# Two layers of a hybrid decoder: router logits in the cross output projection, expert rows gathered and scattered by index, x and y moved by thirds

## The reference

```
x += W_out[pool | MLA | GLA] of RMSNorm(x)
x += CrossAttn(RMSNorm(x))          # 4 heads of 128 over 256 memory tokens, then w_xo
x += HierMoE(RMSNorm(x))
y  = RMSNorm(x)                      # after the last layer

HierMoE(h):
  g_logit = h @ w_rg + b_rg ; group = argmax over 4
  e_logit = h @ w_re + b_re ; the 8 experts of that group ; top 2
  gate    = softmax(g)[group] * top_p / sum(top_p)
  rows of each expert in blocks of 128
  out     = (silu(xb @ w_eg[e]) * (xb @ w_eu[e])) @ w_ed[e]    # 1024 -> 256 -> 1024
  y       = sum over a token's two slots of gate * out
```

## Time and profile before

| | us |
|---|---|
| median of 3 runs (lowest, highest) | 3118.25 (3117.82, 3120.85) |
| the profiled execution | 3119.8 |
| its span, first to last instruction | 3118.0 |
| PE busy in the span | 2694.3 (86%) |
| DVE, ACT, POOL busy | 1239.8 (40%), 748.5 (24%), 335.0 (11%) |
| expert blocks of a layer, first gate/up to the last down, layer 0 | 1122.0 to 1507.8 |

### The profile page before, as it was taken

One profiled execution on the slowest core, in us unless ns is written; L12 is line 12 of the kernel. 1 busy time (PEld: TensorE's weight loads), 2 busy tenths in 40 slices (PEclk: granted clock), 3 DMA queues, 4 the chain that ended last, 5 costly groups with the idle time before them and its releaser, 6 DMA issues.

```text
span 3118.0 us, 33197 instructions
## 1 busy us (share of the span) xinstructions
PE 2694.3 (86%) x12924; PEld 1624.3 (52%) x12924; DVE 1239.8 (40%) x2242; ACT 748.5 (24%) x1513; POOL 335.0 (11%) x499
## 2 busy tenths in 40 slices
PE   7999977789999669999599998668899984999994
PEld 4645556456567334444365455555666752444443
DVE  3155557341313613333343455663223334333325
ACT  1124445231012111111211344443200211111112
POOL 0003324100000010000200232321000002000002
PEclk9999985799999779999799999758899996999996
DMA  9310000331140279998420100005213105899954
GB/s 368 119 27 19 8 31 1 146 129 68 33 156 14 88 307 354 359 356 345 158 70 11 27 13 5 31 4 215 103 34 122 68 22 200 317 360 356 351 230 167
DMA packets 79382, 451.69 MB, mean 145 GB/s; under 512 B 17246, under 2 KB 17884, under 8 KB 67932
## 3 DMA queue, kind: packets, MB, share of 16 engines
q1 hardware_dynamic: 46524, 311.84, 27.0%
q0 software_dynamic: 20368, 101.72, 8.5%
q10 hardware_dynamic: 12352, 36.25, 2.9%
HBM read 361.77 MB, written 84.66 MB: 143 GB/s over the span
## 4 chain that ended last, share of the span: by engine, by line
PE 67%; DVE 18%; ACT 5%; POOL 4%; issue 3%; DMA 2%; ACTq 0%; DVEq 0%; POOLq 0%; SPq 0%
PE ps L612 18%; PE ps L1187 15%; PE ps L1127 4%; PE ps L649 4%; PE ps L729 4%; DVE arena L2206 4%; DVE arena L2200 3%; PE ps L741 2%; PE ps L906 2%; PE ps L757 2%; PE ps L818 2%; DVE arena L1642 2%; PE ps L707 2%; POOL slots L2345 1%; PE ps L955 1%
## 5 line engine op out<-in xcount | busy, mean ns | idle before, releaser
L612 PE MATMUL ps<-arena,ring 128*128 128x352 f32 x1920 | 574.0, 462 | 2.3 <-ACTq L400 1.0
L612 PEld LDWEIGHTS ps<-arena,ring 128*128 128x128 f32 x1920 | 366.4, 191 | 207.7 <-issue 5.0
L1187 PE MATMUL ps<-arena 128*128 128x512 f32 x1024 | 463.6, 606 | 11.6 <-DVE arena L2200 5.6
L1187 PEld LDWEIGHTS ps<-arena 128*128 128x128 f32 x1024 | 191.9, 192 | 245.8 <-issue 225.1
L1205 PE MATMUL ps<-arena 128*128 128x512 f32 x512 | 232.2, 596 | 3.2 <-ACT arena L1572 3.2
L2205 DVE TENSOR_SCALAR arena<-arena 128x256 f32<-128x256 f32 x64 | 18.8, 294 | 496.9 <-ACT arena L1568 496.9
L729 PE MATMUL ps<-arena 96*128 96x512 f32 (+3 forms) x384 | 149.7, 500 | 0.0
L2016 DVE TENSOR_TENSOR x<-x,ps 128x1056 f32<-128x1056 f32 x32 | 40.1, 1255 | 274.8 <-PE ps L612 199.0
L1205 PEld LDWEIGHTS ps<-arena 128*128 128x128 f32 x512 | 93.0, 191 | 97.6 <-issue 93.9
L1579 ACT ACTIVATE arena<-ps 128x1024 f32<-128x1024 f32 x64 | 65.6, 1024 | 259.9 <-PE ps L1205 259.9
L2358 POOL DMA_INDIRECT arena<-slots,dest x36 | 37.5, 1041 | 814.7 <-ACTq L400 804.3
(11 more groups left out here) (375 smaller groups left out, 3742.8 us busy)
## 6 DMA issues: line engine op xcount, KB each, us to landing
arena<-in_w_e SPq DMA_DIRECT2D x64, 3072.0 KB, 11.1
arena<-slots SPq DMA_DIRECT2D x64, 512.0 KB, 4.4
slots<-arena ACTq DMA_DIRECT2D x64, 512.0 KB, 10.3
ring<-in_ring SPq DMA_DIRECT2D x56, 512.0 KB, 3.7
slots<-arena POOLq DMA_DIRECT2D x1, 24576.0 KB, 81.4
arena<-in_mem_k SPq DMA_DIRECT2D x16, 512.0 KB, 6.5
arena<-in_mem_v SPq DMA_DIRECT2D x16, 512.0 KB, 9.9
x<-in_x SPq DMA_DIRECT2D x1, 4224.0 KB, 15.7
```

The costliest lines, as they stand in the source:

```text
L612: mm = pe.matmul(ps[:, (j % 2) * NCH + c, 0:CH], ring[:, slot, (j % per) * units + k, :], src[:, k, tok], start=k == 0, stop=k == units - 1)
L1187: mm = pe.matmul(ps[:, 2, :], xb_t[:, p, k, :], w_e[j][:, k * 512:(k + 1) * 512], start=k == 0, stop=k == KT - 1)
```

## The change

1. The router's logits are accumulated within the cross output projection. After tile j of x is final, ACT writes its square and, scaled by the gain g_ffn alone, the tile itself to `xn`; after the projection matmuls of tile j+1 PE adds tile j's part to the logits (`logits`). The root of the mean square is found once per token, and the logits are multiplied by it afterwards on DVE, where the bias is added too. Barrier 8 is gone.
2. The rows are transposed unnormalised, and ACT multiplies by the token's factor as it copies them to `xr`. SP writes them in token order to a DRAM tensor `xrow`; nothing waits for the routing there.
3. Nine more matmuls give each token's place with the counts of earlier tiles included. Two comparisons and 18 matmuls then turn token -> slot into a table slot -> token, `idx`: for each block a column of 128 row numbers; a slot that holds nobody gets a number outside the bounds, and that row isn't moved.
4. In the expert blocks POOL gathers the rows of a block from `xrow` by that table (`gather`, in place of `load_x`) and scatters y to `yrow` (`scatter`, in place of ACT's store); `release` tells ACT that a y buffer has been written out. `slots`, its zero fill and the waits for it are gone.
5. In the combine stage the two rows of a token lie at fixed places of `yrow`, so SP loads them with plain DMAs, one per tile.
6. x is loaded and y stored in three parts, one per chunk of tokens, and each chunk's work waits only for its own part (the masks load with the second, rope with the third).

```diff
-        slots = nc.dram_tensor("slots", [NBLK * CAP, D], F32).ap()
+        xrow = nc.dram_tensor("xrow", [TOK, D], F32).ap()
+        yrow = nc.dram_tensor("yrow", [2 * ROWS, D], F32).ap()
...
+            def x_load(c):
+                sp.dma_start(x[:, :, chunks[c][1]], ins["x"][:, :, chunks[c][1]]).then_inc(x_moved[c], 16)
             sp.dma_start(consts[:, :], ins["consts"]).then_inc(setup, 16)
-            sp.dma_start(rope[64:96, :, :], ins["rope"]).then_inc(setup, 16)
-            sp.dma_start(lmask_f, ins["lmask"]).then_inc(setup, 16)
-            sp.dma_start(x[:, :, :], ins["x"]).then_inc(setup, 16)
             sp.dma_start(pages[:, :], ins["pages"]).then_inc(setup, 16)
+            x_load(0)
+            sp.dma_start(lmask_f, ins["lmask"]).then_inc(x_moved[1], 16)
+            x_load(1)
+            x_load(2)
+            sp.dma_start(rope[64:96, :, :], ins["rope"]).then_inc(x_moved[2], 16)
...
-                def load_x(p, n):
-                    sp.dma_start(xb[:, p, :], slots[bass.ds(CAP * n, CAP), :]).then_inc(xb_full[p], 16)
...
+                sp.wait_ge(states_stored, 16 * (DB + 6 + 2 * GH))
+                sp.wait_ge(lin_done, IN_MT + OUT_MT + XK_MT + XQ_MT + 1)
                 load_w(0, 0)
-                sp.wait_ge(ssq_ready, 3 * NCH)
-                load_w(3, 3)
-                sp.wait_ge(rows_ready, 1)
-                load_x(0, 0)
-                load_x(1, 1)
-                sp.wait_ge(xr_done, NT + 1)
-                load_w(1, 1)
-                load_w(2, 2)
-                for n in range(2):
-                    sp.wait_ge(tx_done, n + 1)
-                    load_x(n, n + 2)
+                for t in range(NT + 1):
+                    m = P if t < NT else ND
+                    sp.wait_ge(xr_evac, t + 1)
+                    sp.dma_start(xrow[t * P:t * P + m, :], xr[0:m, t % 4, :]).then_inc(row_moved[t % 4], 16)
+                sp.wait_ge(ssq_ready, 2 * NCH + 1)
+                sp.wait_ge(tabled, 1)
+                for j in range(1, 4):
+                    load_w(j, j)
...
-                        sp.wait_ge(tx_done, n + 3)
-                        sp.sem_inc(turn, 1)
-                        load_x(j % 2, n + 4)
                         sp.wait_ge(dn_done, n + 1)
                         sp.sem_inc(turn, 1)
                         load_w(j, n + 4)
...
+                for t in range(NT + 1):
+                    m = P if t < NT else ND
+                    if t >= 4:
+                        sp.wait_ge(c_ready, t - 3)
+                    sp.dma_start(yg[0:m, t % 4, :, :], yrow.rearrange("(s r) d -> r s d", s=2)[t * P:t * P + m, :, :]).then_inc(row_moved[t % 4], 16)
...
+            for c, tok in chunks:
+                sp.wait_ge(norm_ready, c + 1)
+                sp.dma_start(outs["y"][:, :, tok], xn[:, :, tok]).then_inc(x_moved[c], 16)
+            for c in range(NCH):
+                sp.wait_ge(x_moved[c], loaded[c] + 16)
...
+                def logits(k):
+                    pe.wait_ge(xg_ready, k + 1)
+                    if k == 0:
+                        pe.wait_ge(wr_full, 16)
+                    for c, tok in chunks:
+                        mm = pe.matmul(lg_at[c], w_r[:, k, :], xn[:, k, tok], start=k == 0, stop=k == KT - 1, skip_group_check=True)
+                        if k == KT - 1:
+                            mm.then_inc(lg_done, 1)
                 for j in range(XO_MT):
                     for c in range(NCH):
                         if j == 0 and c == NCH - 1:
                             x_back(NT)
                         x_out(j, c)
-                stage_end(pe, 8)
+                    if j >= 1:
+                        logits(j - 1)
+                logits(KT - 1)
                 pe.wait_ge(sq_added, 2)
...
+                for t in range(NT + 1):
+                    m = P if t < NT else ND
+                    mm = pe.matmul(ps[0:m, 2, t:t + 1], xsum[:, t * P:t * P + m], ones[:, 0:1], start=True, stop=True)
+                mm.then_inc(ssq_ready, 1)
...
+                for t in range(6):
                     rows_of(t)
                 pe.wait_ge(both_ready, 1)
...
+                pe.matmul(ps[:, 4, 0:(NT + 2) * NE], con("below"), both.rearrange("p t e -> p (t e)"), start=True, stop=False,
+                          skip_group_check=True)
+                for t in range(NT + 1):
+                    mm = pe.matmul(ps[:, 4, (t + 1) * NE:(NT + 2) * NE], ones,
+                                   both[:, t, :].unsqueeze(1).broadcast_to([P, NT + 1 - t, NE]), start=False, stop=t == NT,
+                                   skip_group_check=True)
+                mm.then_inc(ranked, 1)
+                for t in range(6, NT + 1):
                     rows_of(t)
+                for s_ in range(2):
+                    pe.wait_ge(hot_ready, s_ + 1)
+                    for t in range(NT + 1):
+                        mm = pe.matmul(ps[:, 5, 0:NBLK], hot_row[:, s_, t, :], hot_blk[:, s_, t, :], start=s_ + t == 0,
+                                       stop=s_ == 1 and t == NT)
+                mm.then_inc(tabled, 1)
...
+                    act.wait_ge(lin_evac, IN_MT + OUT_MT + XK_MT + XQ_MT + k + 1 + 2)
+                    act.activation(xsum if k == 0 else xsq[:, k % 2, :], x[:, k, :], ACT.Square, scale=D ** -0.5).then_inc(sq_ready, 1)
+                    act.activation(xn[:, k, :], x[:, k, :], ACT.Copy, scale=gain("g_ffn", k)).then_inc(xg_ready, 1)
                 for c, tok in chunks:
                     act.wait_ge(lg_done, c + 1)
...
+                    act.activation(lgt[0:NR, tok], lg_at[c], ACT.Copy).then_inc(lg_evac, 1)
+                act.wait_ge(ssq_ready, 2 * NCH + 1)
+                act.activation(rstd_t[:, 0:NT], ps[:, 2, 0:NT], ACT.Sqrt, bias=EPS).then_inc(std_ready, 1)
+                act.activation(rstd_t[0:ND, NT:NT + 1], ps[0:ND, 2, NT:NT + 1], ACT.Sqrt, bias=EPS).then_inc(std_ready, 1)
...
+                for t in range(NT + 1):
                     m = P if t < NT else ND
                     act.wait_ge(xr_done, t + 1)
                     if t >= 4:
...
                     b = 0 if t % 2 == 0 else 6
-                    act.activation(xr[0:m, t % 4, :].rearrange("p (a n) -> p a n", a=2), ps[0:m, b:b + 2, :], ACT.Copy).then_inc(xr_evac, 1)
...
+                    act.activation(xr[0:m, t % 4, :].rearrange("p (a n) -> p a n", a=2), ps[0:m, b:b + 2, :], ACT.Copy,
+                                   scale=rstd_t[0:m, t:t + 1]).then_inc(xr_evac, 1)
...
-                def send_y(n, p, sent):
+                def keep_y(n, p):
                     act.wait_ge(dn_done, n + 1)
-                    act.wait_ge(y_sent[p], sent + 16)
+                    act.wait_ge(y_out, n + 1)
                     act.sem_inc(turn, 1)
                     act.activation(y_sb[:, p, :].rearrange("p (a n) -> p a n", a=2), ps[:, 4:6, :], ACT.Copy).then_inc(dn_evac, 1)
-                    act.wait_ge(dn_evac, n + 1 + 1)
-                    act.sem_inc(turn, 1)
-                    act.dma_start(slots[bass.ds(CAP * n, CAP), :], y_sb[:, p, :]).then_inc(y_sent[p], 16)
...
+                for j in range(KT):
+                    dve.wait_ge(lin_done, IN_MT + OUT_MT + XK_MT + XQ_MT + j + 1)
+                    xs = x[:, j, :].rearrange("p (c n) -> p c n", c=NCH)
+                    dve.tensor_tensor(xs, xs, ps[:, (j % 2) * NCH:(j % 2 + 1) * NCH, 0:CH], ALU.add).then_inc(lin_evac, 1)
+                    if j >= 2:
+                        add_xsq(j - 1)
+                add_xsq(KT - 1)
...
+                for s_ in range(2):
+                    step(dve.tensor_tensor(hot_blk[:, s_], blk_f[:, s_, :].unsqueeze(2).broadcast_to([P, NT + 1, NBLK]),
+                                           iota[:, 0:NBLK].unsqueeze(1).broadcast_to([P, NT + 1, NBLK]), ALU.is_equal))
+                    step.mark(dve.tensor_tensor(hot_blk[:, s_], hot_blk[:, s_], row_id[:, s_, :].unsqueeze(2).broadcast_to([P, NT + 1, NBLK]),
+                                                ALU.mult))
+                    step.sync()
+                    dve.tensor_tensor(hot_row[:, s_], row_f[:, s_, :].unsqueeze(2).broadcast_to([P, NT + 1, P]),
+                                      iota.unsqueeze(1).broadcast_to([P, NT + 1, P]), ALU.is_equal).then_inc(hot_ready, 1)
+                dve.wait_ge(tabled, 1)
...
+                dve.tensor_copy(idx, table).then_inc(idx_ready, 1)
...
-            pool.dma_start(slots.rearrange("(p n) (f c) -> p (n f) c", p=P, c=512),
-                           zeros.unsqueeze(1).broadcast_to([P, NBLK * CAP // P * 2, 512])).then_inc(slots_clear, 16)
...
+                def gather(n):
+                    pool.indirect_dma_start(xb[:, n % 2, :], None, xrow, bass.IndirectOffsetOnAxis(ap=idx[:, 0, n:n + 1], axis=0),
+                                            bounds_check=TOK - 1, oob_is_err=False).then_inc(xb_full[n % 2], 16)
+                def scatter(n):
+                    pool.wait_ge(dn_evac, n + 1 + 1)
```

(58 more changed lines are left out.)

177 lines of the change are left out of this document (64 added, 113 removed).

## The result

| | us |
|---|---|
| before, median of 4 runs beside it (lowest, highest) | 3118.03 (3116.57, 3120.85) |
| changed, median of 4 runs (lowest, highest) | 3544.95 (3539.55, 3548.68) |
| ratio, 95% interval | 1.136 (1.134 to 1.138) |
| changed, the profiled execution and its span | 3547.88, 3546.0 |

The change is slower by 427 us. 3383 had been forecast, within 3265 to 3550.

A forecast was written before the change was run, and what follows sets the result against it. PE, busy 86% of the span, was taken as the bound, its own in the expert blocks. Sum: 3119.8 + 307 (expert blocks) - 30 (logits, table, first gather) - 6 (start) - 6 (end) - 2 (combine) = 3383 us, range 3265 to 3550.

The forecast's parts named there:

- the clock's case: Expert blocks: rival that PE's clock falls after each stall, each costing 2.6 us more, 151 in all, 3534; chance 0.13.
- The rule of the queue: Expert blocks: gather(n+1), behind scatter(n-2) on POOL, cannot issue before block n-2's down matmuls end; 5.3 us a block, 58 times.
- T: Start of a block's gate/up matmuls; the forecast counts times within a block from it, the old period being 11.77 us.
- The expert blocks: Both layers: late gathers lengthen the period from 11.77 to 17.05 us, 58 x 5.3 = +307; this forecast had chance 0.47.
- the middle of two rows: Expert blocks: gather landing taken as T+12.15, between the y store's T+11.55 and the x load's T+12.8.
- the crowded engines: Expert blocks: rival that filled rows crowd on some DMA engines, gather landing at T+12.8, 58 x 5.9 = 342, 3418; chance 0.17.
- Logits in the projection, table, first gather: Last residual add to first gate/up: logits within the projection, row scatters gone; -15 us a layer, -30 in all (-10 to -50).
- Combine: Combine stage: one SP load a tile replaces two POOL issues, last scatter takes POOL's path; -2 us in all (-6 to +4).
- Start: Kernel start: with x in thirds, two squares and sums are done before the last third's; -6 us (-3 to -9).
- end: Kernel end: only a third of the 11.8 us from the y store's issue is left; -6 us (-4 to -8).
- Zero fill: nothing: First projection: removing the zero fill gains nothing, as its 352 matmuls take 104.40 us with or without it.

The follow-up runs named there:

- The later scatter: Changed kernel with POOL's queue in the order gather(n+2), scatter(n-2), the scatter two blocks later: 3088.04 us, 0.991 of the kernel before.
- the run with spread rows: Changed kernel with slot r of a block in partition 2r, then the odd ones, instead of partition r: 3466.72 us, ratio 1.110.
- the filled wait: Changed kernel with six more 128x512 matmuls a block between gate/up and the transposes of x, output unchanged: 3421.51 us (one run).
- The run with the first weights held back: Scatter two blocks later, plus SP loading weights of blocks 1 to 3 only after gathers 0 and 1 land: 3057.03 us, ratio 0.982.

## Why the prediction was right, and where it was not

**The direction and the mechanism held, the size did not.** 3545 us lies only 5 us inside the range, whose upper end was there for the clock's case alone, with a chance of 0.13; the forecast itself was 162 us too low. The rule of the queue (a gather behind a scatter that waits for y cannot leave before T) and its times were right to 0.2 us: gather from T+3.2 to T+4.3, forecast T+3.1 to T+4.1; 58 stalls. The later scatter took it all away.

**The expert blocks were mis-sized: +447, not +307.** Two things, and both were listed as rivals. I took the landing from the middle of two rows, T+12.15; it came at the upper end, T+12.7, and the transposes began at T+12.95, 0.7 later than by my sum. I had charged the crowded engines as a case of their own, and the run with spread rows shows that they take part. The larger error was the clock. The argument against it, that a gap of 2.63 us had left the clock at 1.00, was an argument from a short gap to one twice as long; the filled wait shows 2.1 us of the 7.7 per block to be the clock alone. The rival's price of 2.6 a stall was near the 2.4 measured, but it is the transposes and down that pay it; gate/up, 7.03 us, runs at 1.00. The rivals were priced as if only one could be true; crowded engines and clock together, 342 + 151, would have been +493, and the truth lies between. From the rows: 326 us of stalls and 139 for the slower matmuls behind them are 465. Against these 18 too many stand 7 us less of idle time ahead of gate/up (11.6 before, 4.6 now) and 7 less of gate/up itself (busy 463.6 before, 456.3 now); the last few are not accounted for.

**Logits in the projection, table, first gather: -15 a layer was -12.3 in layer 0.** The parts were off both ways. The changed kernel's timeline:

```profile
1034.74 1.25 DVE L2154 TENSOR_TENSOR x<-x,ps 128x1056 f32<-128x1056 f32 x1 [6.18 <-PE ps L1138]
...
1045.56 0.50 DVE L2165 TENSOR_TENSOR arena<-arena 128x324 f32<-128x324 f32 x1
...
1079.20 1.10 POOL L2391 DMA_INDIRECT arena<-xrow,arena  x1 [162.98 <-DVE arena L2237]
...
1101.06 1.97 PE L1212 MATMUL ps<-consts,arena 128*128 128x128 f32 x8 [23.71 <-POOLq L409]
```

With the start's 5.2 us added back, the last residual add comes at 1039.9: the projection grew by 7, not 13 (six logit matmuls take 1.37 us there, not 6 x 0.307). Logits are ready at 1051.3, forecast 1056. The indices took 32 us from there (33), so gather 0 left POOL at 1079.2, where 1091 less the start's 5 had been forecast. From the last add to the first gate/up the timelines have 19.3 us less, where 28 had been named. The 7 us at the gather and 3 more were lost again behind it: the first gathers were forecast to land in at most 10.4 us and took up to 20.3, beside three weight loads at once, and gate/up began at 1104.5. The run with the first weights held back won some 30 us of that for the two layers.

In layer 1 the gain after the last add is nearly the same (-17.9, against -19.3 in layer 0), but 5 us are lost in the middle of the layer, where no code was changed: the granted clock is 0.88 in the changed kernel between 2306 and 2506 us and 0.91 in the matching 200 us before. The run with the later scatter, with the same code there, is 3 us shorter from the end of the first combine to the last add of layer 1. The cause was not followed up.

**Combine: -2 was +9.** I had priced the loads and not what comes before them (layer 1):

```profile
3466.23 1.02 ACT L1610 ACTIVATE arena<-ps 128x1024 f32<-128x1024 f32 x1 [3.90 <-PE ps L1238]
3468.03 0.97 POOL L2397 DMA_INDIRECT yrow<-arena  x1 [4.18 <-ACT arena L1610]
3477.58 2.12 SPq L586 DMA_DIRECT2D arena<-yrow  x4
```

From the start of ACT's last copy of y to the first load are 11.35 us; in the kernel before 5.3 to the first gather (5.4 in layer 0). By the first transposes of the combine 4.7 and 4.5 us of the difference are left (layers 0 and 1), which are the 9.

**Start -5.2 and end -5.7 were right in size (-6, -6).** "Zero fill: nothing" was right for the kernel before, where everything waited for all of x anyway and the 352 matmuls take 104.40 us with and without it. But the start's gain exists only because the fill is gone. The two terms are one.

## What to carry to other kernels

When a queue issues two kinds of work, ask of each entry what the entry ahead of it waits for: a store that waits for the end of a block must not stand ahead of the load that the next block needs, and moving it back costs nothing where the buffers allow it. Price a stall on TensorE together with the matmuls behind it, and do not treat causes that can hold together as cases that exclude each other. A gain may need two edits at once, and an edit that is free in the old kernel can be what releases it.

## What the runs showed of the hardware

- PE idle for some 5.6 us in each 20 brought the work behind the stall to the lower level: x transposes 1.97 us for 1.04, down matmuls up to 5.75 for 3.60, granted clock 0.50 from the transposes on and 1.00 again in gate/up, 0.83 on the mean between 1284 and 1325 us. With PE busy in the wait it was 1.00 throughout.
- A gather of some 66 rows lands in 4.3 to 4.8 us (medians, and the first two of the run with the gathers first) when no weight transfer is asked for just before it, in 9.5 beside one and in 12.9 to 20.3 beside three. Its landing follows the transfers that it travels beside, not its own bytes.
- A barrier let PE through 0.2 us after the landing of POOL's last gather, at 1098.2 and at 1082.6 us: POOL's drain had waited for it.
